# A fused three-layer transformer kernel: where the norms' squares are summed, how q and k leave PSUM, heads in pairs, and VectorE's order at stage borders

## The reference

```python
x = x + mixer(rms_norm(x, mix_norm[i]))      # i = 0: attention with window + short conv; i = 1: gated linear attention
x = x + conv_ffn(rms_norm(x, ffn_norm[i]))   # (gelu(conv(h @ w_up)[:, :2816]) * conv(...)[:, 2816:]) @ w_down
x = x + sigmoid(rms_norm(x, ple_norm[i]) @ w_gate) * (p[i] @ w_proj)
```

## Time and profile before

| | |
|---|---|
| three timed runs, median | 1127.4 us (1125.84 to 1128.56) |
| profiled execution | 1129.37 us |
| its span | 1127.6 us, 21949 instructions |
| PE busy | 1089.9 us |
| VectorE busy | 829.6 us |
| ScalarE busy | 647.1 us |
| GpSimd busy | 59.2 us |

### The profile page before, as it was taken

The page is one execution under the profiler, slowest core; times in us unless marked ns, Lnnn a source line. Parts: engine busy times, 40 slices in busy tenths (PEclk is TensorE's granted clock), DMA queues, the critical chain, the costliest instruction groups (busy, mean ns, idle before and its releaser), DMA issues.

```text
span 1127.6 us, 21949 instructions
## 1 busy us (share of the span) xinstructions
PE 1089.9 (97%) x8800; PEld 1065.9 (95%) x8800; DVE 829.6 (74%) x1011; ACT 647.1 (57%) x886; POOL 59.2 (5%) x41
## 2 busy tenths in 40 slices
PE   6989999999999998999999999998999999999998
PEld 6978999999999998987999999997999999999997
DVE  6668775566666755888888887377887878888456
ACT  6556652555444436535687775365446578776452
POOL 1200010010000002000100000022000100000020
PEclk9999999999999999999999999999999999999999
DMA  8932355444555563532455556543442445555641
GB/s 313 226 112 96 129 194 181 134 140 155 185 182 186 187 224 112 186 113 76 158 184 181 186 195 225 187 172 112 150 150 76 170 167 185 176 187 189 222 166 40
DMA packets 29416, 186.37 MB, mean 165 GB/s; under 512 B 3511, under 2 KB 5784, under 8 KB 7592
## 3 DMA queue, kind: packets, MB, share of 16 engines
q1 hardware_dynamic: 29352, 185.45, 48.2%
HBM read 184.09 MB, written 1.34 MB: 164 GB/s over the span
## 4 chain that ended last, share of the span: by engine, by line
PE 80%; DVE 11%; DMA 3%; ACT 3%; issue 2%; SPq 0%; ACTq 0%; DVEq 0%
PE g L453 56%; PE d L453 24%; DVE w_lo L1188 4%; DMA raw<-weights 2%; DVE a_lo L1192 2%; ACT w_hi L837 1%; DVE b_lo L1192 1%; PE d L456 1%; DVE x L1185 1%; DMA bias_dram<-bias_rows 1%; DVE newton L1182 0%; DVE newton L1192 0%; SPq L414 0%; DMA x<-x_t 0%; DVE x L1192 0%
## 5 line engine op out<-in xcount | busy, mean ns | idle before, releaser
L1188 DVE TENSOR_TENSOR w_lo<-raw,w_hi 128x2048 fp32r<-128x2048 f32 (+1 forms) x171 | 389.3, 2279 | 96.7 <-ACT w_hi L837 96.6
L837 ACT ACTIVATE w_hi<-raw 128x2048 fp32r<-128x2048 f32 (+1 forms) x171 | 323.4, 1896 | 126.5 <-PE d L453 90.1
L453 PE MATMUL g<-a_hi,w_hi 128*128 128x256 f32 x1232 | 354.6, 288 | 16.3 <-DVE w_lo L1188 11.0
L453 PE MATMUL g<-a_lo,w_hi 128*128 128x256 f32 x1232 | 350.1, 284 | 0.0
L453 PE MATMUL g<-a_hi,w_lo 128*128 128x256 f32 x1232 | 350.0, 284 | 0.0
L453 PEld LDWEIGHTS g<-a_hi,w_hi 128*128 128x128 f32 x1232 | 237.7, 193 | 20.8 <-DVE w_lo L1188 12.5
L453 PEld LDWEIGHTS g<-a_lo,w_hi 128*128 128x128 f32 x1232 | 237.9, 193 | 0.1
L453 PEld LDWEIGHTS g<-a_hi,w_lo 128*128 128x128 f32 x1232 | 237.7, 193 | 0.0
L453 PE MATMUL g<-b_hi,w_hi 128*128 128x256 f32 x672 | 192.0, 286 | 5.0 <-DVE w_lo L1188 4.3
L453 PE MATMUL g<-b_lo,w_hi 128*128 128x256 f32 x672 | 190.1, 283 | 0.0
L453 PE MATMUL g<-b_hi,w_lo 128*128 128x256 f32 x672 | 190.1, 283 | 0.0
(11 more groups left out here) (272 smaller groups left out, 1401.0 us busy)
## 6 DMA issues: line engine op xcount, KB each, us to landing
raw<-weights SPq DMA_DIRECT2D x169, 1024.0 KB, 4.8
bias_tab<-bias_dram SPq DMA_DIRECT2D x8, 192.0 KB, 9.5
x<-x_t SPq DMA_DIRECT2D x4, 256.0 KB, 5.8
raw<-weights SPq DMA_DIRECT2D x2, 512.0 KB, 5.6
mem_t<-mem_t SPq DMA_DIRECT2D x1, 1024.0 KB, 13.0
out<-x SPq DMA_DIRECT2D x4, 256.0 KB, 2.3
p_in<-p_t SPq DMA_DIRECT2D x2, 256.0 KB, 5.1
level_mask_f<-level_mask SPq DMA_DIRECT2D x1, 512.0 KB, 5.2
```

Source lines behind the costliest of these rows:

```text
L453: return pe.matmul(out, lhsT, rhs, start=start, stop=stop, skip_group_check=True)
L837: return act.activation(out, in_, func, **kw)
L1188: return dve.tensor_tensor(out, a, b, ALU.subtract)
```

## The change

The squares stay in four buffers each; VectorE adds them (`add_squares`) and adds the two halves (`halve_squares`), and `norm_sum` is one matmul. GpSimd keeps only its memsets. At the opening of a stage both engines first make the weights of chunks 2 and 3 ready (`opening`) and norm after that; PE sums after chunk 1 instead of chunk 0. In `residual` and `down` VectorE splits the activations before the weights. The memory's norm is summed together with the MoBA heads'. ScalarE reads q and k of the hybrid mixer from PSUM, unscaled, and squares them there; the token's scale enters through eps (`hy_eps`). `score_tiles` fills two banks in turn, `weigh_values` takes heads in pairs with three banks for the transposes. Several evictions, weight splits and the load of `const` change their place. The diff, cut to its core (first PE and SP, then ScalarE, VectorE, GpSimd):

```diff
+            load(1, 1)
             sp.dma_start(const[:], io["const"]).then_inc(got_const, 16)
-            load(1, 1)
...
-            def norm_sum(sums=sq_sum):
+            def norm_sum(squares=SQUARES, bank=STAT):
 
                 pe.wait_ge(sq_total, count.next(sq_total))
-                acquire(STAT)
-                mm(D[STAT][:, 0:T], ones, sums[:, 0:T], True, False)
-                fill(STAT, mm(D[STAT][:, 0:T], ones, sums[:, T:2 * T], False, True), full_dve, mean_done)
+                acquire(bank)
+                fill(bank, mm(D[bank][:, 0:T], ones, squares[0][:, 0:T]), full_dve, mean_done)
 
             def outputs(name, moving):
 
                 def body(j, jm):
-                    fresh = isinstance(j, int) and j == 0
-                    chunk(name, j, jm, moving, fresh)
-                    if fresh:
+                    early = isinstance(j, int)
+                    chunk(name, j, jm, moving, fresh=early and j == 0)
+                    if early and j == 1:
...
                 if j == 2:
                     turn_scale(rstd, 1)
-                if j == 4:
-                    norm_sum()
...
             def score_tiles(q, key, q0, t):
 
-                keys = (t + 1) * P
-                for b in range(4 if t else 2):
-                    acquire(b)
-                    for i, m in enumerate(maps_of(b, t)):
-                        half = slice((m % 2) * 64, (m % 2) * 64 + 64)
-                        last = mm(D[b][:, i * keys:(i + 1) * keys], q[half, q0 + m // 2, t * P:(t + 1) * P], key(m)[half, 0:keys])
-                    fill(b, last, full_dve, drained_dve)
+                keys, per_bank = (t + 1) * P, 2 if t else 4
+                for pair in range(0, 4 if t else 2, 2):
+                    for b in (pair, pair + 1):
+                        acquire(b)
+                    for i in range(per_bank):
+                        for b in (pair, pair + 1):
+                            m = maps_of(b, t)[i]
+                            half = slice((m % 2) * 64, (m % 2) * 64 + 64)
+                            last = mm(D[b][:, i * keys:(i + 1) * keys], q[half, q0 + m // 2, t * P:(t + 1) * P], key(m)[half, 0:keys])
+                            if i == per_bank - 1:
+                                fill(b, last, full_dve, drained_dve)
 
             def weigh_values(heads, values, place_of, per_bank, probs, probs_t):
 
                 turned = {}
-                for step in range(heads + 1):
-                    if step < heads:
-                        b = step % 2
-                        acquire(b)
-                        for i in range(3):
-                            last = turn(D[b][:, i * P:(i + 1) * P], probs[:, step, i * P:(i + 1) * P])
-                        turned[step] = fill(b, last, full_act, drained_act)
+                for step in range(heads // 2 + 1):
+                    if step < heads // 2:
+                        for h in (2 * step, 2 * step + 1):
+                            b = TURN_BANKS[h % 3]
+                            acquire(b)
+                            for i in range(3):
+                                last = turn(D[b][:, i * P:(i + 1) * P], probs[:, h, i * P:(i + 1) * P])
+                            turned[h] = fill(b, last, full_act, drained_act)
                     if step >= 1:
-                        h = step - 1
-                        b = 2 + h // per_bank
-                        to = place_of(h)
-                        pe.wait_ge(*turned[h])
-                        if h % per_bank == 0:
+                        pair = (2 * step - 2, 2 * step - 1)
+                        b = 2 + pair[0] // per_bank
+                        for h in pair:
+                            pe.wait_ge(*turned[h])
+                        if pair[0] % per_bank == 0:
                             acquire(b)
-                        mm(to, values(0, h), probs_t[:, h % 4, 0:T], True, False)
-                        last = mm(to[:, P:T], values(1, h), probs_t[:, h % 4, T:3 * P], False, True)
-                        if h % per_bank == per_bank - 1:
+                        for h in pair:
+                            mm(place_of(h), values(0, h), probs_t[:, h % 4, 0:T], per_bank == 4 or h == pair[0], False)
+                        for h in pair:
+                            last = mm(place_of(h)[:, P:T], values(1, h), probs_t[:, h % 4, T:3 * P], False, True)
+                        if pair[1] % per_bank == per_bank - 1:
...
-            turn_scale(rstd_mem, W_IN_Q + 1)
...
-            pe.wait_ge(sq_for_pe, count.next(sq_for_pe, 2))
+            pe.wait_ge(sq_total, count.next(sq_total, 2))
             acquire(STAT)
-            for f in range(4):
-                last = mm(D[STAT][:, 0:T], ones, sq[:, f // 2, (f % 2) * T:(f % 2 + 1) * T], f == 0, f == 3)
-            fill(STAT, last, full_dve, mean_done)
+            mm(D[STAT][:, 0:T], ones, sq[:, 0, 0:T])
+            fill(STAT, mm(D[STAT][:, T:2 * T], ones, sq_sum[:, 0:T]), full_dve, mean_done)
...
+            for h in range(4):
+                pe.wait_ge(evicted, FIRST_OUT["w_cq"] + h + 1)
...
-                if j < 2:
-                    norm_sum((sq_sum, gain_sq_sum)[j])
+                if j == 1:
+                    norm_sum()
+                    norm_sum(GAIN_SQUARES, 2)
             tiles_of = (2, 2, 1)
-            for i in range(3):
-                pe.wait_ge(sq_for_pe, count.next(sq_for_pe))
+            pe.wait_ge(sq_for_pe, count.next(sq_for_pe, 3))
+            for i in (2, 0, 1):
...
-            for j in (4, 5, 6):
+            for j in (4, 5):
                 chunk("hy_in", j, j % U, A)
             pe.wait_ge(qk_rotated, count.next(qk_rotated))
             acquire(STAT)
-            pe.wait_ge(*fill(STAT, mm(D[STAT][:, 0:T], swap_half, hy_qk[:, 4, :]), full_act, drained_act))
+            keys_swapped = fill(STAT, mm(D[STAT][:, 0:T], swap_half, hy_qk[:, 4, :]), full_act, drained_act)
+            chunk("hy_in", 6, 0, A)
+            pe.wait_ge(*keys_swapped)
...
+            def opening(name):
+
+                ahead(name, 0, 0)
+                ahead(name, 1, 1)
+                rough_rstd()
...
+            def queries_and_keys(i):
+
+                act.wait_ge(chunk_done, FIRST["hy_in"] + i + 1)
+                bank = G[(FIRST_OUT["hy_in"] + i) % U]
+                tiles = slice(2 * i, min(2 * i + 2, 5))
+                fn(flat(hy_rot[:, tiles, :]), bank[:, 0:(tiles.stop - tiles.start) * T], ACT.Square).then_inc(sq_for_pe, 1)
+                for f in range(tiles.start, tiles.stop):
+                    gain = pcol("hy_k_norm_2" if f == 4 else "hy_q_norm_2")
+                    last = fn(hy_qk[:, f, :], bank[:, (f % 2) * T:(f % 2 + 1) * T], scale=gain)
+                last.then_inc(evicted if i < 2 else qk_gained, 1)
...
+                hy_ahead(8 - t)
...
+                    if j < 3:
+                        ahead(f"gate{layer}", j + 1, (j + 1) % U)
...
+            gla_ahead(10)
...
+            def add_squares(first, last, squares=SQUARES):
+
+                for i in range(first, last):
+                    dve.wait_ge(sq_done, count.next(sq_done))
+                    if i > 1:
+                        dve.wait_ge(dve_own, count.sent[dve_own])
+                    if i > 0:
+                        add(squares[0], squares[0], squares[i]).then_inc(dve_own, count.one(dve_own))
+
+            def halve_squares(squares=SQUARES):
+
+                dve.wait_ge(dve_own, count.sent[dve_own])
+                add(squares[0][:, 0:T], squares[0][:, 0:T], squares[0][:, T:2 * T]).then_inc(sq_total, 1)
+
+            def opening(name):
+
+                ahead(name, 0, 0)
+                ahead(name, 1, 1)
+                token_norm()
...
-                    ahead(name, j, j % U)
                     dve.wait_ge(evicted, count.sent[evicted])
                     prep_pair(moving, gain, g0, x, j)
+                    ahead(name, j, j % U)
+                    add_squares(j, j + 1)
+                halve_squares()
...
+            evict("w_in", W_IN_Q, W_IN_Q % U, pair_at(qkv, W_IN_Q), split=False)
             dve.wait_ge(got_bias, 16 * P // SKEW)
             for t, cols in score_tiles(scores, lambda maps, c: bias_tab[:, maps.start:maps.stop:2, c]):
                 negate_max(scores, t, cols)
-            turned_scale(rstd_mem_tok)
+                if t == 1:
+                    ahead("w_in", W_IN_Q, W_IN_Q % U)
             reciprocals(1)
             normalise(scores, 1, TILE1, 2 * P).then_inc(dve_own, count.one(dve_own))
+            evict("w_in", 7, 1, pair_at(qkv, 7), split=False)
             reciprocals(0)
             normalise(scores, 0, TILE0, P).then_inc(probs_done, 1)
-            for j in (7, 8, 9):
-                first_chunk(j)
-            mean(STAT, 4 * P)
+            ahead("w_in", 7, 1)
+            evict("w_in", 8, 2, pair_at(qkv, 8), split=False)
+
+            dve.wait_ge(att_squared, count.next(att_squared, 2))
...
+                    if b > 0:
```

(92 more changed lines are left out.)

237 lines of the change are left out of this document (122 added, 115 removed).

## The result

The kernel after takes 1110.8 us (median of four runs, 1109.4 to 1112.6) where the kernel before takes 1127.5: ratio 0.9854, 95% interval 0.9835 to 0.9873, or 16.7 us less (14.3 to 18.6). Forecast were 1107.7 and 19.7 us. The profiled execution took 1110.52 with a span of 1108.7, 18.9 less than the span of before.

What follows compares the result with a forecast made beforehand. PE, 97% busy, was the bound, gaining only where it idles, mostly waiting for VectorE, or has fewer matmuls. Gains 9.0 + 7.5 + 4.1 + 2.4 = 23.0, less 3.3, gave 19.7 off 1127.4: 1107.7 us, range 1100 to 1117.

Steps and rivals of the forecast that it cites:

- first mixer, to w_out: First mixer, 55 to 141 us: earlier scores, paired heads and smaller pieces were to save 9.0 us.
- hybrid mixer with its borders: 442 to 549 us: 5.3 up to the first scores, 1.7 to the transposes, 2.0 behind, less 1.5: gain 7.5.
- gate to GLA: Embedding gate and GLA opening, 740 to 786 us: 41.1 us for 45.2, gain 4.1, one idle piece of about 3 left.
- ordinary borders, last gate, gla_out: Other stage borders, the conv layers, last gate and gla_out: earlier splits and shorter sums, less losses, gain 2.4 us.
- bias and clock, charged apart: Two costs not placed exactly: 1.6 us for the later bias_rows store and 1.7 for one clock drop, 3.3 together.
- The clock: Half-clock intervals behind idle pieces at 57 to 60 and at 501 counted as gone; one new drop charged, 1.7 us.
- The bias path: bias_rows' store, queued ahead of chunk 7's load, starts some 3.4 us later: cost -0.7 to +3.2, taken as 1.6.
- The heads: Eight first-mixer heads in pairs, column halves fully overlapping because the order alternates: 6.3 us for 10.2, gain 3.9.
- The hybrid heads: Hybrid mixer: the same gain from pairing heads, nearly all hidden by VectorE's taps.
- Down to hybrid mixer: Border at 442 us: splits without GpSimd beside them gain 5.0; 5.3 counted up to the first score matmul.
- the conv stages: Conv layers: chunk 4's w_lo done at 24.3 where PE asks at 23.5, 0.85 back, net -0.3 in each.
- The slower rival: VectorE's 26 us of adds all land on the path if they stand before the split PE needs: 1134 us, chance 0.03.

Runs made afterwards that it cites:

- e3: The kernel after, with VectorE's refining of the moba and memory norms and scaling of att_a moved behind the first mixer's last token eviction: 1104.8 us.
- e11: The kernel after, unchanged, timed again in a second comparison with the kernel before: 1108.8 us against 1129.0, ratio 0.9831.
- e2: The kernel after, with the four value matmuls of a pair of heads ordered 1, 1, 2, 2 instead of 1, 2, 1, 2: 1108.9 us.
- e8: The kernel before, with only the heads taken in pairs (transposes and values, on TensorE and ScalarE): 1121.0 us.
- e12: The kernel before, with only the adds of the squares moved to VectorE, right behind the activation splits, other orders as before: 1135.6 us.
- e1: The kernel after, with GpSimd again adding the squares of the x and memory norms and TensorE summing both halves: 1118.3 us.

## Why the prediction was right, and where it was off

The sign, the range and the mechanism held. Of the signs of being right, one failed: PE was to idle under 6 us in the hybrid mixer, and it idles 7.0 of 100.2. Of the signs of being wrong, two came. There are more than two half-clock intervals, and PE waits at a residual chunk for w_lo, 1.60 at 520.42, which the sum had charged. Term by term, by the starts of the same chunks in the two traces:

| stretch | forecast | measured |
|---|---|---|
| first mixer, to w_out | 9.0 | 6.1 |
| hybrid mixer with its borders | 7.5 | 8.3 |
| gate to GLA | 4.1 | 2.1 |
| ordinary borders, last gate, gla_out | 2.4 | 2.2 |
| bias and clock, charged apart | -3.3 | in the rows above |
| sum | 19.7 | 18.8 |

**The clock is the step that was mis-sized.** I counted the two half-clock intervals of before (60.65, 501) as gone with the idle time and charged one new one, 1.7. After has three in front of its last matmul, two in the first mixer and one at the gate. Those are the misses of the first and third row: 1.6 us at the differential heads (e3 removes exactly this and the 3.3 of idle), 1.5 at 60, and 1.6 at the gate, which in e11 runs without its interval and gains 3.7 for the 4.1 forecast.

**The reference was mis-sized too.** The profiled execution of before, whose waits I added up, had a clock of 0.996; the commonest value of before is 0.998, with 1126.1 to 1128.4 us. At 0.996 before takes 1128.5 to 1129.7 and after 1108.5 to 1109.4 (three executions), some 20 us less. But the two executions around after's median had 0.995 and 0.994. Savings that I saw in an execution with two intervals were taken off the median of executions that mostly lack one of them, so its removal was counted though the median had nothing to remove; that is 1.9 of the 2.2 between 18.9 in the traces and 16.7 in the medians. Only the profiled executions show their intervals; for the others their number is worked out from the granted clock. e11's chip, where before stood at 0.996 in its median execution, shows 20.2.

**The bias path** was charged with 1.6 and cost nothing. Its store left 2.9 us later and chunk 7's load was issued at 37.92 instead of 36.40, but ScalarE got the weights at 51.99, where the load ended at 52.19 before.

**The heads** took 6.38 us for the 6.3 of full overlap: right number, and the reason I gave ("the order alternates") wrong, by e2. The Trainium skill (TensorE: Matmul & The Clock Gate, Measured speedup vs the span model), by whose 2.38 for three column tiles I had 6.7, gives no figure for two halves, and its ratio does not carry over: two heads' values take 0.87 as one head's did. **The hybrid heads** "nearly all hidden": 2.2 of 3.4 us were not, by e8.

**Down to hybrid mixer:** 5.2 us up to the swapped keys against 5.3. The waits named as handed back came as forecast: 1.96 in front of the hybrid transposes (2.3), 3.39 idle in front of the differential heads (3.3), 3.46 at the GLA chunk (about 3), 1.52 in hy_out's residual (1.5). In the conv stages 1.43 came back, not 0.85: ScalarE finished the w_hi of chunk 4, behind the table load and the first Gelu, at 554.42, so its w_lo was done 24.8 us behind the stage's start and not 24.3, and PE's restart takes its part; net -1.3 and -0.7 for the -0.3 forecast in each.

**The slower rival** ("VectorE becomes the bound") had the right condition, adds ahead of what PE needs next, and the wrong size of chance: e12, which moves the squares and leaves the order as it was, meets it in one place and is slower than before. The move pays only with its order. By e1 the squares' place is worth 7.5 us in the finished kernel, by e8 the heads 6.7 in the old one. These two are not parts of one sum, and what the orders and q and k through ScalarE would bring by themselves was not run.

## What to carry to other kernels

When an engine's work is moved to one that is already last at the borders, check each place for who asks next: the adds cost nothing where they stood behind the split that TensorE wanted, and in one place where TensorE wanted their sum first they cost 8.4 us of waiting and half clock behind it. Idle time in front of TensorE can cost twice, since the clock may fall behind it; here an idle piece of 3 us cost 3 to 5. And compare a profiled execution with a median only with the granted clock of both beside them. The same holds for a gain at one place: subtract the half-clock interval that one trace has there and the other has not.

## What the hardware showed that was not expected

- Two instructions with SBUF inputs on VectorE and GpSimd excluded each other for whole instructions, both ways: a GpSimd add of 1.3 us took 3.3 beside a w_lo of 2.3. An input from PSUM (0.68) or a memset was free of it.
- Matmuls for the two column halves ran side by side, and not in the order of the queue: in e2 the third (second head) started 0.013 us behind the first, the second (first head again) 0.48 us behind it.
- Executions of one kernel differ by how many half-clock intervals they have, in the traces mostly 3.41 us long: the kernel before took 1125.9 to 1126.6 us at a clock of 1.0, 1126.1 to 1128.4 at 0.998 and 1132.3 at 0.993. The same kernel waited 3.18 us in front of the first GLA chunk's products in after and 3.21 in e11; a half-clock interval followed in the first and none in the second.
